# A streaming encoder step on one core: first weight quarter loaded one K tile at a time, fourteen products of ones at the start

## The chip, the cores and the metric

The kernel runs on one core of a Trainium2 chip. A core has a matrix engine (TensorE, PE in the profile, its weight loads PEld), a vector engine (VectorE, DVE), an activation engine (ScalarE, ACT), a general engine (GpSimd, POOL) and a synchronizing engine (SyncE, SP), each with its own instruction queue, and 16 DMA engines. The metric is the device time of one execution in microseconds (us), as the median of several.

## The reference, cut to what matters

One layer of a hybrid encoder for 512 prompt tokens and 8 x 16 sample tokens, 640 in all. Everything is float32.

```
h = rmsnorm(x) @ w_in              # 2048 -> 8448, split into u, z_a, q, k, v, z_b, g_a, g_b
branch_A = GLU(gelu(S5(u))) * silu(z_a)
branch_B = attention(q, k, v) * silu(z_b)
y = x + (sig(g_a) * (branch_A @ w_out_a) + sig(g_b) * (branch_B @ w_out_b)) @ w_o
```

The change lies in the first thing computed: the products of x with the first two blocks of 128 columns of w_in (the first quarter of u). The row factor of the norm is applied to the results, so these products can start before the sums of squares are known.

## The kernel before, in words

All weight matrices are cut into 102 units of 128 x 2048 numbers. A unit of w_in's first eight holds 16 K tiles of 128 x 128. A product in full precision is made of three products in a rounded format: each operand is split into a high part (its rounded value) and a low part (what the rounding left), and hi*hi, lo*hi and hi*lo are added in PSUM. ScalarE makes w_hi by a copy from the raw weights, GpSimd makes w_lo = raw - w_hi, both for every unit. For x, ScalarE makes x_hi (with the norm's gain), and VectorE makes x_lo. x is 16 tiles of 128 x 640, kept for all the input units.

The first three units are handled by quarters of 512 columns, that is of four K tiles. SyncE's queue (L363 to L372) issues, for each quarter, the quarter of unit 0, that of unit 1, and four x tiles; then the quarters of unit 2, each once the old content of its buffer has been split. Units 3 and later go whole.

ScalarE's loop over the 16 x tiles (L997 on) copies the two weight quarters at k = 0, 4, 8, 12, then x_hi of the tile; from k = 8 on it adds the square of x tile k - 8 (`SQ_LAG`). After the loop come the squares of tiles 8 to 11, then the two copies that empty the accumulators of units 0 and 1 (`u_raw`, they raise `acc_free`), the last quarter of unit 2, and the squares of 12 to 15. A square waits for VectorE's running sum two tiles back. VectorE's loop makes x_lo of tile k and from k = 8 on adds the square of tile k - 8 to `ssum`; then come the last eight sums. GpSimd makes the w_lo quarters in the order of the loads (`low`, L451).

TensorE (L521 on) goes over the 16 K tiles of units 0 and 1 together: six products of 320 columns for each unit and tile, weights stationary. It waits for the unit's w_lo quarter (`part_split`, for the last one `w_split`) and for x_lo of the tile (`x_split`). Then unit 2 runs alone and has first to wait for `acc_free` 1. At its tile 8 `norm_sums` multiplies the finished `ssum` with a 128 x 128 tile of ones; from that the roots come on VectorE and ScalarE, and behind the roots in ScalarE's queue stands the copy of unit 3's weights. All later units follow on TensorE one after the other.

The semaphores that the change renumbers are `part_hi` (quarters copied by ScalarE), `part_split` (quarters split by GpSimd) and `x_loaded[k]` (16 for each transfer). `prep` counts GpSimd's two fills, `ones` first.

Of the kernel before, what the change touches and what calls it, by code (L numbers as in the profile page):

```python
# [59 lines left out]
U_ZG = 22  # L60
ZGS = 3
SQ_LAG = 8
SSM_BANK = (6, 7, 5, 6)
KV_BANK = (0, 1, 4, 2, 3)
BRB_AT = ((), (), (0, 1), (2, 3), (4, 5), (6, 7), (), ())
# [25 lines left out]
def build(nc, xT, gain, wts, cst, onehot, rel_tab, sinks, sinks_s, a_re, a_im, log_dt, b_re, b_im, c_re, c_im,  # L91
# [150 lines left out]
    with ctx:  # L242
# [114 lines left out]
        @block.sync  # L357
        def _(spe):
            def load(n, slot):
                spe.dma_start(raw[slot][:], wts[ds(n, 1)].rearrange("a p n -> (a p) n")).then_inc(w_loaded[slot], 16)  # L360

            for q in range(4):
                for p in range(2):  # L363
                    spe.dma_start(raw[p][:, quarter(q)], wts[p][:, quarter(q)]).then_inc(part_loaded[2 * q + p], 16)
                for k in range(4 * q, 4 * q + 4):
                    spe.dma_start(x_raw[:, k, :], xT[k]).then_inc(x_loaded[k], 16)
            for q in range(4):
                if q < 3:
                    spe.wait_ge(part_split, 2 * q + 1)
                else:  # L370
                    spe.wait_ge(w_split, 1)
                spe.dma_start(raw[0][:, quarter(q)], wts[2][:, quarter(q)]).then_inc(part_loaded[8 + q], 16)  # L372
            for t, src in ((tab, rel_tab), (hot, onehot)):
                spe.dma_start(t[:], src).then_inc(small_loaded, 16)
            spe.wait_ge(w_split, 2)
            load(3, 1)
            for t, src in ((sp["are"], a_re), (sp["aim"], a_im), (bre, b_re), (bim, b_im), (cre, c_re),
                           (cim, c_im), (dsk, dskip), (bcol, bglu), (qgc, qg), (kgc, kg),
                           (ident, cst[0]), (diag, cst[2][:, 0:CH])):
                spe.dma_start(t[:], src).then_inc(ssm_loaded, 16)  # L380
            for g2 in range(2):
                spe.dma_start(sp["dt"][64 * g2:64 * g2 + 64, :],
                              log_dt[g2:g2 + 1, :].broadcast_to([64, PAIRS])).then_inc(ssm_loaded, 16)
                spe.dma_start(sk[64 * g2:64 * g2 + 64, :], sinks[g2:g2 + 1, :].broadcast_to([64, 8])).then_inc(ssm_loaded, 16)
            for h in range(8):
                spe.dma_start(skS[16 * h:16 * h + 16, :], sinks_s[h:h + 1, :].broadcast_to([16, 2])).then_inc(ssm_loaded, 16)

            def next_unit(n, p):
                spe.wait_ge(w_split, n - 1)
                load(n, p)  # L390

            spe.wait_ge(prep, 2)
            for kv in range(2):
                spe.dma_start(k_scr[kv, :, 0:PAD], zeros[0:HD, :]).then_inc(pads_stored, 16)
            spe.dma_start(v_scr[0:PAD, :], zeros[:]).then_inc(pads_stored, 16)
            for p in range(2):
                next_unit(4 + p, p)
            spe.wait_ge(rel_copied, 1)
            spe.dma_start(f_scr, fsb[:].unsqueeze(1).broadcast_to([16, QC, RELW])).then_inc(f_stored, 16)

            def store_c(i):

                spe.wait_ge(mats_ready, i + 1)
                for r in range(2):
                    for g2 in range(2):
                        spe.dma_start(c_scr[r].rearrange("p (j a) n -> a p j n", a=2)[g2][:, ds(BLK * i, BLK)],
                                      powers[64 * g2:64 * g2 + 64, :, 0, r, CH:(STEP + 1) * CH]).then_inc(c_stored, 16)

            def load_u(s):
                spe.dma_start(U[16 * (7 - s):16 * (8 - s)],  # L410
                              u_scr.rearrange("t (g c) (s k) -> s c (t g) k", g=8, s=STEP)[s]).then_inc(u_loaded, 16)

            for n in range(6, 18):
                next_unit(n, n % 2)
                if n in C_AT:
                    store_c(C_AT.index(n))
            spe.wait_ge(blk_stored, 32 * 4)
            spe.wait_ge(c_stored, 64 * 4)
            for p in range(2):
                spe.wait_ge(u_stored[p], 64)  # L420
            for p in range(2):
                for s in range(4 * p, 4 * p + 4):
                    load_u(s)
                next_unit(18 + p, p)
            for b in range(2):
                spe.dma_start(Bst[b][:], b_scr[:, BLK * b:BLK * b + BLK]).then_inc(bst_loaded[b], 16)
            with spe.Fori(10, U_G // 2 + 1) as i:
                for p in range(2):
                    next_unit(2 * i + p, p)
            with spe.Fori(0, 7) as c:  # L430
                for k in range(4):
                    next_unit(U_G + 2 + 4 * c + k, k % 2)
                spe.wait_ge(y_done, c + 1)
                stage_h(spe.dma_start, c + 1)
                spe.wait_ge(gelu_stored, 128 * c + 128)
                load_y(spe.dma_start, c + 1)
            with spe.Fori(U_G // 2 + 15, N_UNITS // 2) as i:
                for p in range(2):
                    next_unit(2 * i + p, p)


        @block.gpsimd
        def _(pool):

            for k, (part, value) in enumerate(((ones[:], 1.0), (zeros[:], 0.0))):
                if k:
                    pool.wait_ge(prep, k)
                nc.gpsimd.memset(part, value).then_inc(prep, 1)

            def low(p, cols=slice(0, D)):  # L450
                return nc.gpsimd.tensor_tensor(w_lo[p][:, cols], raw[p][:, cols], w_hi[p][:, cols].bitcast(F32),  # L451
                                               ALU.subtract)

            pool.wait_ge(prep, 2)
            for q in range(4):
                for p in range(2):
                    if q < 3:
                        pool.wait_ge(part_hi, 2 * q + p + 1)
                    else:
                        pool.wait_ge(w_hi_done, p + 1)  # L460
                    low(p, quarter(q)).then_inc(part_split if q < 3 else w_split, 1)
            for q in range(4):
                if q < 3:
                    pool.wait_ge(part_hi, 6 + q + 1)
                else:
                    pool.wait_ge(w_hi_done, 3)
                low(0, quarter(q)).then_inc(part_split if q < 3 else w_split, 1)
            pool.wait_ge(w_hi_done, 4)
            low(1).then_inc(w_split, 1)
            with pool.Fori(2, N_UNITS // 2) as i:  # L470
                for p in range(2):

                    pool.wait_ge(w_hi_done, 2 * i + p + 1)
                    low(p).then_inc(w_split, 1)
# [3 lines left out]
        def _(pe):  # L478
# [32 lines left out]

            def parts_of_unit2(k):
                if k in (0, 4, 8):
                    pe.wait_ge(part_split, 6 + k // 4 + 1)
                if k == 12:
                    pe.wait_ge(w_split, 3)
                if k == 8:
                    norm_sums()


            for k in range(KT):  # L521
                for p in range(2):
                    if k in (0, 4, 8):
                        pe.wait_ge(part_split, 2 * (k // 4) + p + 1)
                    if k == 12:
                        pe.wait_ge(w_split, p + 1)
                    pe.wait_ge(x_split, k + 1)
                    last = k_tile(acc(p), p, k, 0, KT, x_tiles)
                    if k == KT - 1:
                        last.then_inc(proj_done, 1)  # L530
                    elif k % 4 == 3 and p == 0:
                        last.then_inc(part_used, 1)
# [429 lines left out]
        def _(act):  # L962
            def A(out, in_, func, **kw):
                return nc.scalar.activation(out, in_, func, **kw)  # L964
# [30 lines left out]
                    A(sq[k % 2][:], x_raw[:, k, :], ACT.Square).then_inc(x_sq, 1)  # L995

            for k in range(KT):  # L997
                if k % 4 == 0:
                    q = k // 4
                    for p in range(2):  # L1000
                        act.wait_ge(part_loaded[2 * q + p], 16)
                        A(w_hi[p][:, quarter(q)], raw[p][:, quarter(q)], ACT.Copy).then_inc(part_hi if q < 3 else w_hi_done, 1)
                if k >= KT - 2:
                    hi_part2(k - KT + 2)
                if k == 0:
                    act.wait_ge(gain_loaded, 16)
                act.wait_ge(x_loaded[k], 16)
                A(x_hi[:, k, :], x_raw[:, k, :], ACT.Copy, scale=gcol[:, k:k + 1]).then_inc(x_hi_done, 1)
                if k >= SQ_LAG:
                    square_x(k - SQ_LAG)  # L1010
# [1080 lines left out]
```

## Time and profile before

| | us |
|---|---|
| median of 3 runs (lowest, highest) | 1533.71 (1533.5, 1534.25) |
| the profiled execution | 1534.2 |
| its span | 1532.4 |
| TensorE busy | 1520.2 |
| VectorE busy | 654.0 |
| GpSimd busy | 483.9 |
| ScalarE busy | 425.9 |

The span goes from the first to the last instruction; the execution's own time has 1.8 us more around it. A matmul's end is modelled, so records overlap; what counts is the distance between their starts. A row of the timeline may merge several like instructions (x4) and gives in brackets how long the engine was idle before and what ended that.

### The profile page before, as it was taken

How to read it: one execution, taken by the hardware profiler on the slowest of the kernel's cores; microseconds unless marked ns; L12 is line 12 of the kernel's file. 1: busy time of each engine (PE TensorE's matmuls, PEld its weight loads, DVE VectorE, ACT ScalarE, POOL GpSimd, SP SyncE). 2: the span in 40 equal slices, each digit the busy share in tenths (PEclk: the TensorE clock that was granted, in tenths of full speed). 3: DMA queues.
4: the chain of work that ended last, by engine and by line, in shares of the span. 5: the costliest groups of instructions: out<-in, count | busy, mean ns of one | idle time of the engine just before them, and what ended most of it. 6: DMA issues, size and time to landing. Idle time of an engine off the chain costs nothing.

```text
span 1532.4 us, 21441 instructions
## 1 busy us (share of the span) xinstructions
PE 1520.2 (99%) x8377; PEld 1289.6 (84%) x8377; DVE 654.0 (43%) x1049; ACT 425.9 (28%) x582; POOL 483.9 (32%) x117
## 2 busy tenths in 40 slices
PE   7999999999999999999999999999999999999999
PEld 7999888998888878887787877879988888888887
DVE  7897771238776142433424334256522232500000
ACT  7412332421211314323332332434411112311110
POOL 4333232323323232322322323224323333333331
PEclk9999999999999999999999999999999999999999
DMA  7524449743324454464545555446424414342340
GB/s 279 143 76 161 138 141 178 227 142 105 117 83 138 135 147 120 113 164 136 136 114 136 137 145 138 123 167 228 152 83 151 151 56 150 117 151 83 127 148 35
DMA packets 169361, 209.60 MB, mean 137 GB/s; under 512 B 107825, under 2 KB 127569, under 8 KB 155601
## 3 DMA queue, kind: packets, MB, share of 16 engines
q1 hardware_dynamic: 63840, 133.85, 28.8%
q10 hardware_dynamic: 105456, 74.83, 16.6%
q8 instruction: 48, 0.79, 0.2%
q14 instruction: 17, 0.13, 0.0%
HBM read 163.25 MB, written 42.76 MB: 134 GB/s over the span
## 4 chain that ended last, share of the span: by engine, by line
PE 98%; issue 1%; POOL 0%; DMA 0%; DVE 0%; ACT 0%; SPq 0%; POOLq 0%; ACTq 0%
PE ps L795 43%; PE ps L931 14%; PE ps L484 14%; PE ps L798 11%; PE ps L581 9%; PE ps L708 1%; PE ps L717 1%; PE ps L734 1%; PE ps L688 1%; PE ps L732 1%; PE ps L756 1%; PE ps L562 1%; PE ps L724 0%; POOL w_lo L451 0%; PE ps L739 0%
## 5 line engine op out<-in xcount | busy, mean ns | idle before, releaser
L451 POOL TENSOR_TENSOR w_lo<-raw,w_hi 128x2048 fp32r<-128x2048 f32 (+1 forms) x111 | 483.3, 4356 | 1023.8 <-ACT w_hi L964 1023.8
L964 ACT ACTIVATE w_hi<-raw 128x2048 fp32r<-128x2048 f32 (+1 forms) x111 | 197.3, 1778 | 626.3 <-PE ps L798 356.8
L795 PE MATMUL ps<-x_hi,w_hi 128*128 128x512 f32 x704 | 281.9, 400 | 0.0
L795 PE MATMUL ps<-x_lo,w_hi 128*128 128x512 f32 x704 | 274.4, 390 | 0.0
L795 PE MATMUL ps<-x_hi,w_lo 128*128 128x512 f32 x704 | 274.3, 390 | 0.0
L795 PEld LDWEIGHTS ps<-x_hi,w_hi 128*128 128x128 f32 x704 | 132.2, 188 | 30.0 <-issue 1.8
L795 PEld LDWEIGHTS ps<-x_hi,w_lo 128*128 128x128 f32 x704 | 132.1, 188 | 28.4
L795 PEld LDWEIGHTS ps<-x_lo,w_hi 128*128 128x128 f32 x704 | 132.3, 188 | 26.0
L931 PE MATMUL ps<-w_hi,mix_hi 128*128 128x512 f32 x320 | 124.6, 389 | 0.0
L931 PE MATMUL ps<-w_hi,mix_lo 128*128 128x512 f32 x320 | 124.5, 389 | 0.0
L931 PE MATMUL ps<-w_lo,mix_hi 128*128 128x512 f32 x320 | 124.5, 389 | 0.0
L484 PE MATMUL ps<-x_hi,w_hi 128*128 128x320 f32 x384 | 89.5, 315 | 8.6 <-DVE x_lo L1499 8.4
L1992 DVE TENSOR_TENSOR Y<-ps,Y 128x512 f32<-128x512 f32 x20 | 13.6, 692 | 188.0 <-PE ps L931 188.0
L1972 DVE TENSOR_TENSOR gate_in<-ps,gate_in 128x512 f32<-128x512 f32 x40 | 26.7, 692 | 151.8 <-PE ps L795 151.8
L484 PE MATMUL ps<-x_lo,w_hi 128*128 128x320 f32 x384 | 88.5, 312 | 0.0
L484 PE MATMUL ps<-x_hi,w_lo 128*128 128x320 f32 x384 | 88.4, 312 | 0.0
L964 ACT ACT_TABLE_LOAD x37 | 47.5, 1283 | 144.9 <-issue 79.1
L581 PE MATMUL ps<-w_hi,x_hi 128*128 128x512 f32 (+1 forms) x240 | 85.4, 356 | 0.0
L581 PE MATMUL ps<-w_hi,x_lo 128*128 128x512 f32 (+1 forms) x240 | 84.9, 354 | 0.0
L581 PE MATMUL ps<-w_lo,x_hi 128*128 128x512 f32 (+1 forms) x240 | 84.9, 354 | 0.0
L484 PEld LDWEIGHTS ps<-x_hi,w_hi 128*128 128x128 f32 x384 | 65.0, 191 | 9.2 <-POOL w_lo L451 8.8
L1856 DVE SCALAR_TENSOR_TENSOR Sb<-ps,bias 128x768 f32<-128x768 f32 x16 | 15.3, 958 | 133.1 <-PE ps L717 133.1
(267 smaller groups left out, 2535.2 us busy)
## 6 DMA issues: line engine op xcount, KB each, us to landing
raw<-in_wts SPq DMA_DIRECT2D x99, 1024.0 KB, 5.0
g_scr<-gbuf ACTq DMA_DIRECT2D x8, 1024.0 KB, 8.1
gate_in<-g_scr ACTq DMA_DIRECT2D x8, 1024.0 KB, 6.2
x_raw<-in_xT SPq DMA_DIRECT2D x16, 320.0 KB, 8.3
Y<-in_x_tok ACTq DMA_DIRECT2D x20, 256.0 KB, 4.7
out_y_tok<-Y ACTq DMA_DIRECT2D x20, 256.0 KB, 2.8
c_scr<-powers SPq DMA_DIRECT2D x16, 256.0 KB, 4.3
b_scr<-bT ACTq DMA_DIRECT2D x4, 1024.0 KB, 5.7
```

Of the source, the lines that this page charges most:

```text
L451: return nc.gpsimd.tensor_tensor(w_lo[p][:, cols], raw[p][:, cols], w_hi[p][:, cols].bitcast(F32), ALU.subtract)
L484: last = nc.tensor.matmul(outs[:, h, :], w[p][:, c:c + P], act[k][:, h * HALF:(h + 1) * HALF], start=(k == 0 and w is w_hi and act is hi), ...
L562: last = nc.tensor.transpose(ps[:, SSM_BANK[part], (2 * j + ri) * P:(2 * j + ri + 1) * P], powers[:, 2 * part + j, 1, ri, 0:P], ident[:])
L581: last = nc.tensor.matmul(out, act, w[p][:, c:c + width], start=(k == 0 and act is hi and w is w_hi), stop=(k == KT - 1 and act is lo))
L688: last = nc.tensor.matmul(ps[64 * g2:64 * g2 + 64, 4 + 2 * (b % 2) + j // 2, col:col + NCH], Bst[b // 2 % 2][:, 4 * (b % 2) + j, ri, 64 * ...
L708: last = nc.tensor.matmul(out, mat[:, g, m:m + HD], src[:, g, :], start=mat is Mst, stop=mat is Cst)
L717: last = nc.tensor.matmul(ps[:, 5 + r, j * BAND:(j + 1) * BAND], Qp[rows, 2 * j:2 * j + 2, :].rearrange("p a q -> p (a q)"), Kb[rows], sta ...
L795: last = nc.tensor.matmul(ps[:, bank, :], w[p][:, col + P * i:col + P * i + P], act[:, 0:PROMPT], start=opens, stop=final and w is w_lo)
L798: last = nc.tensor.matmul(ps[:, bank, :], act[:, PROMPT:TOK], w[p][:, col:col + WB], start=opens, stop=final and w is w_lo)
L931: last = nc.tensor.matmul(ps[:, t, :], act, w[p][:, c:c + WB], start=(k == 0 and act is hi and w is w_hi), stop=(k == KT - 1 and act is lo))
L964: return nc.scalar.activation(out, in_, func, **kw)
L1972: v.tensor_tensor(g, ps[:, (5 * h + i) % 8, :], g, ALU.mult).then_inc(out_free, 1)
```

## The change

The first quarter of units 0 and 1 is no longer loaded, copied and split as 512 columns, but as four pieces of 128 columns, one for each K tile. SyncE issues piece k of unit 0, piece k of unit 1 and x tile k, for k = 0 to 3; ScalarE copies the two pieces and then x_hi; GpSimd splits eight pieces of 128 columns; TensorE waits for each piece. Pieces 1 to 3 share the semaphore of their x tile, which then counts 48. All later counts are raised accordingly. And ahead of its first operands TensorE makes fourteen products of the tile of ones with itself (128 columns, plain float32) into a PSUM bank that nothing reads, as soon as `prep` is 1.

```diff
+WARM = 14
...
-            for q in range(4):
+            for k in range(4):
+                for p in range(2):
+                    spe.dma_start(raw[p][:, P * k:P * k + P], wts[p][:, P * k:P * k + P]).then_inc(
+                        x_loaded[k] if k else part_loaded[p], 16)
+                spe.dma_start(x_raw[:, k, :], xT[k]).then_inc(x_loaded[k], 16)
+            for q in range(1, 4):
                 for p in range(2):
                     spe.dma_start(raw[p][:, quarter(q)], wts[p][:, quarter(q)]).then_inc(part_loaded[2 * q + p], 16)
                 for k in range(4 * q, 4 * q + 4):
                     spe.dma_start(x_raw[:, k, :], xT[k]).then_inc(x_loaded[k], 16)
             for q in range(4):
                 if q < 3:
-                    spe.wait_ge(part_split, 2 * q + 1)
+                    spe.wait_ge(part_split, 2 * q + 7)
...
             pool.wait_ge(prep, 2)
-            for q in range(4):
+            for k in range(4):
+                for p in range(2):
+                    pool.wait_ge(part_hi, 2 * k + p + 1)
+                    low(p, slice(P * k, P * k + P)).then_inc(part_split, 1)
+            for q in range(1, 4):
                 for p in range(2):
                     if q < 3:
-                        pool.wait_ge(part_hi, 2 * q + p + 1)
+                        pool.wait_ge(part_hi, 2 * q + p + 7)
...
-                    pool.wait_ge(part_hi, 6 + q + 1)
+                    pool.wait_ge(part_hi, 12 + q + 1)
...
                 if k in (0, 4, 8):
-                    pe.wait_ge(part_split, 6 + k // 4 + 1)
+                    pe.wait_ge(part_split, 12 + k // 4 + 1)
...
+            pe.wait_ge(prep, 1)
+            for i in range(WARM):
+                nc.tensor.matmul(ps[:, 7, 0:P], ones[:], ones[:], start=True, stop=True)
             for k in range(KT):
                 for p in range(2):
-                    if k in (0, 4, 8):
-                        pe.wait_ge(part_split, 2 * (k // 4) + p + 1)
+                    if k < 4:
+                        pe.wait_ge(part_split, 2 * k + p + 1)
+                    if k in (4, 8):
+                        pe.wait_ge(part_split, 2 * (k // 4) + p + 7)
...
             for k in range(KT):
-                if k % 4 == 0:
+                if k < 4:
+                    if k:
+                        act.wait_ge(x_loaded[k], 48)
+                    for p in range(2):
+                        if k == 0:
+                            act.wait_ge(part_loaded[p], 16)
+                        A(w_hi[p][:, P * k:P * k + P], raw[p][:, P * k:P * k + P], ACT.Copy).then_inc(part_hi, 1)
+                elif k % 4 == 0:
...
-                act.wait_ge(x_loaded[k], 16)
+                if k == 0 or k > 3:
+                    act.wait_ge(x_loaded[k], 16)
```

## Rows read from the trace of the kernel before

**Rows 1.** The page: its head, and busy us, share and instructions of TensorE.
```profile
span 1532.4 us, 21441 instructions
PE 1520.2 (99%) x8377; PEld 1289.6 (84%) x8377; DVE 654.0 (43%) x1049; ACT 425.9 (28%) x582; POOL 483.9 (32%) x117
```

**Rows 2.** The page: the chain that ended last, by engine.
```profile
PE 98%; issue 1%; POOL 0%; DMA 0%; DVE 0%; ACT 0%; SPq 0%; POOLq 0%; ACTq 0%
```

**Rows 3.** Waits of TensorE, whole span: us in total, times, longest.
```profile
PE ps L484 <- DVE x_lo L1499: 8.4, 1, 8.4
```

**Rows 4.** Windows: length, PE busy (records), granted clock, DMA share, GB/s.
```profile
0.00:8.42 8.42, 0.00 (x0) 1.00 0.72 244
8.42:14.30 5.88, 5.88 (x22) 1.00 1.00 370
14.30:38.50 24.20, 24.20 (x166) 1.00 0.76 267
```

**Rows 5.** Timeline of TensorE: start us, length us, instruction, count.
```profile
8.42 0.87 PE L484 MATMUL ps<-x_hi,w_hi 128*128 128x320 f32 x2 [8.42 <-DVE x_lo L1499]
...
39.46 0.56 PE L484 MATMUL ps<-x_hi,w_hi 128*128 128x320 f32 x2
...
47.22 1.34 PE L508 MATMUL ps<-ssum,ones 128*128 128x320 f32 x4
48.40 1.17 PE L541 MATMUL ps<-ones,ssum 128*128 128x1 f32 x10
...
56.87 0.56 PE L484 MATMUL ps<-x_hi,w_hi 128*128 128x320 f32 x2
```

**Rows 6.** Timeline of ScalarE.
```profile
4.33 1.31 ACT L964 ACTIVATE w_hi<-raw 128x512 fp32r<-128x512 f32 x2 [2.09 <-DMA raw<-in_wts]
6.26 3.21 ACT L964 ACTIVATE x_hi<-x_raw,gcol 128x640 fp32r<-128x640 f32 x4 [0.62 <-DMA x_raw<-in_xT]
9.67 0.63 ACT L964 ACTIVATE w_hi<-raw 128x512 fp32r<-128x512 f32 x1 [0.20 <-DMA raw<-in_wts]
...
16.51 0.83 ACT L964 ACTIVATE x_hi<-x_raw,gcol 128x640 fp32r<-128x640 f32 x1 [0.20 <-DMA x_raw<-in_xT]
...
37.16 0.74 ACT L964 ACTIVATE sq<-x_raw 128x640 f32<-128x640 f32 x1 [0.19 <-DVE ssum L1491]
38.70 0.71 ACT L964 ACTIVATE u_raw<-ps 128x640 f32<-128x640 f32 x1 [0.80 <-PE ps L484]
39.58 0.70 ACT L964 ACTIVATE u_raw<-ps 128x640 f32<-128x640 f32 x1 [0.17 <-PE ps L484]
```

**Rows 7.** Timeline of VectorE.
```profile
17.37 2.63 DVE L1499 SCALAR_TENSOR_TENSOR x_lo<-x_raw,gcol,x_hi 128x640 fp32r<-128x640 f32 x2 [1.26 <-ACT x_hi L964]
...
22.19 0.88 DVE L1499 SCALAR_TENSOR_TENSOR x_lo<-x_raw,gcol,x_hi 128x640 fp32r<-128x640 f32 x1
...
23.82 1.82 DVE L1499 SCALAR_TENSOR_TENSOR x_lo<-x_raw,gcol,x_hi 128x640 fp32r<-128x640 f32 x1
...
32.61 1.92 DVE L1499 SCALAR_TENSOR_TENSOR x_lo<-x_raw,gcol,x_hi 128x640 fp32r<-128x640 f32 x1
34.46 4.53 DVE L1491 TENSOR_TENSOR ssum<-ssum,sq 128x640 f32<-128x640 f32 x5
```

**Rows 8.** Timeline of GpSimd.
```profile
0.74 0.20 POOL L448 MEMSET ones<- 128x128 f32 x1 [0.29 <-POOLq L2067]
...
5.11 2.49 POOL L451 TENSOR_TENSOR w_lo<-raw,w_hi 128x512 fp32r<-128x512 f32 x2 [3.90 <-ACT w_hi L964]
...
22.62 6.02 POOL L451 TENSOR_TENSOR w_lo<-raw,w_hi 128x512 fp32r<-128x512 f32 x3 [4.09 <-ACT w_hi L964]
28.85 1.62 POOL L451 TENSOR_TENSOR w_lo<-raw,w_hi 128x512 fp32r<-128x512 f32 x1 [0.21 <-ACT w_hi L964]
...
52.18 4.64 POOL L451 TENSOR_TENSOR w_lo<-raw,w_hi 128x2048 fp32r<-128x2048 f32 x1 [9.99 <-ACT w_hi L964]
```

**Rows 9.** Timeline of SyncE's queue.
```profile
1.65 1.85 SPq L366 DMA_DIRECT2D x_raw<-in_xT  x4
```

**Rows 10.** DMA: x tile 3; unit 2's last quarter; issues at 32.04 and 32.52.
```profile
x_raw<-in_xT SPq DMA_DIRECT2D x1, 320.0 KB, 5.5
...
raw<-in_wts SPq DMA_DIRECT2D x1, 256.0 KB, 3.0
...
kgc<-in_kg SPq DMA_DIRECT2D x1, 0.5 KB, 3.6
ident<-in_cst SPq DMA_DIRECT2D x1, 64.0 KB, 3.3
```

## The prediction

> **What bounds the kernel now.** I read the engine shares first: TensorE (PE) is busy for 1520.2 of the span's 1532.4 us [rows 1], and the chain that ended last is TensorE for 98% [rows 2]. The table of waits has one single wait on the PE row: 8.4 us, the very first, until the first x_lo tile [rows 3]. So whatever the change brings must be a shift of TensorE's whole stream, and it is worth what the stream is earlier by at the first place behind which everything hangs on TensorE itself.
>
> Then the windows: from 8.42 to 14.30 us TensorE starts 22 products of 320 columns in 5.88 us, 267 ns apart; from 14.30 to 38.50 it starts 166 in 24.20 us, 146 ns apart [rows 4]. 320 columns in 267 ns is the lower level, 1.2 GHz; in 146 ns nearly the upper, 2.4 GHz. The granted clock stands at 1.00 in both rows, so only the spacing shows it. The engine had done nothing before. Those 22 products cost 22 x 0.121 = 2.7 us more than they would at the upper level.
>
> Last, the first 60 us engine by engine, because TensorE alone does not say how far the others are behind it. The first product of unit 2 stands at 39.46 [rows 5]. It needs accumulator 0, which ScalarE empties at 38.70 for 0.71 us, after waiting 0.80 us for TensorE [rows 6]. In ScalarE's queue the four squares of x tiles 8 to 11 stand directly ahead of this copy; the last runs from 37.16 to 37.90 and waits for VectorE's running sum [rows 6]. VectorE in turn is busy without a gap that matters from 17.37 to 38.99: x_lo 15 runs 32.61 to 34.53 and five sums 34.46 to 38.99 [rows 7]. It is slow because GpSimd runs its three w_lo of the last quarter and of unit 2 in the same stretch: an x_lo takes 1.82 or 1.92 us there against 0.88 elsewhere [rows 7, 8]. What starts that chain is not TensorE: x_hi 8 at 16.51 came 0.20 us after a wait for its own transfer [rows 6].
>
> **The parts.**
>
> *TensorE's first operands.* They need w pieces 0 of both units and x tile 0. Bytes queued ahead of the end of x tile 0 fall from 256+256+320 KB to 64+64+320 KB. x_hi 0 begins at 6.26 now and TensorE at 8.42, so 2.16 us lie behind the transfer [rows 5, 6]. How much earlier x tile 0 lands no row shows. If bytes set it, 384 KB fewer are worth 1.0 us at the 370 GB/s of the second stretch and 1.6 at the 244 of the first [rows 4]; if the queue's start-up sets it, nothing. I take 1.1 us, since the queue moved bytes all the while: first operands at 7.3 (6.8 to 8.4).
>
> *Fourteen products of ones.* ones is written at 0.94 [rows 8]. Two 320-column products of plain f32 (four records) take 48.40 - 47.22 = 1.18 us at the upper level [rows 5], so 128 columns cost 0.24 us, and 0.43 at the lower level (x 267/146). Fourteen take 3.3 to 6.0 us and end by 7.1, before the operands. They delay nothing. In the trace the level rose 5.9 us after the first product, so 1.1 + 5.9 = 7.0: nearly all of the 2.7 us should be saved.
>
> *Feeding tiles 1 to 15.* At 12 x 0.147 = 1.76 us per K tile, TensorE would want tile k at 7.3 + 1.76k and finish unit 1 at 35.5. ScalarE's two 512-column copies (0.65 each) become eight of 128 columns, at most 0.36 each; GpSimd's two at 1.25 become eight of about 0.43, by the slope between 512 and 2048 columns (4.64 - 1.25 over 1536) [rows 6, 8]. Both fall between x tiles that come 0.8 us or more apart, on engines idle here: ScalarE ended tile 3 at 9.47 and waited for the next quarter, so they cost nothing unless that cover of 0.2 us and the following waits is gone. Up to tile 12 nothing is late. But x_lo 15 ends at 34.53 [rows 7] and is wanted at 33.7: here TensorE starts to wait again, about 1.3 us with d (below) and the 0.14 from x_lo to product.
>
> *The six extra transfers.* SyncE issues 12 instead of 6 before quarter 1, 0.46 us each ([rows 9], four in 1.85 us): its queue moves back 2.8 us. x tile 3 is issued near 0.74 + 11 x 0.5 = 6.3 instead of 3.07, when it lands at 3.07 + 5.5 = 8.6 [rows 10]. A 256 KB transfer issued into a nearly empty queue landed after 3.0 us [rows 10]; with 0.2 for the larger size tile 3 comes at 9.5 at the latest, 0.9 late. From quarter 1 on the transfers stand back to back again and can make none of it up, or some. Small packets cost something too: kgc (landed 3.6 after 32.04) and ident, 64 KB (landed 3.3 after 32.52) are 0.2 us apart, so 64 KB in 512-byte rows take 0.2 us or a little more; eight take 1.9 where two of 256 KB took 1.4 (512 KB at 370 GB/s). Together tiles 4 to 15 come 0 to 0.9 us later (the idle moments of the queue and the 0.5 overlap); between the ends I take d = 0.4. The later issues (unit 2's quarters, unit 3, the SSM constants) wait for GpSimd's counts anyway and keep their times within d.
>
> *Where it is paid out.* ScalarE cannot empty accumulator 0 before the square of tile 11 is done: 37.90 + d. TensorE's first product of unit 2 came 0.76 us after that copy's start (39.46 - 38.70), so it comes at 38.66 + d = 39.06 instead of 39.46. TensorE's unit 1 now ends about 34.9 + 0.1 + 1.8 = 36.8, and it stands still for over 2 us. Of 3.9 us earned, 0.80 - d = 0.4 is left. Even with no products of ones at all the number would be the same: 8.42 - 7.3 = 1.1 is already more than 0.4.
>
> *After it.* Everything later hangs on TensorE. The sums of squares for the norm (47.22) feed the root, the copy of unit 3's weights and its w_lo (52.18 to 56.82), and unit 3 starts at 56.87, as soon as that is done [rows 5, 8]: this chain begins at TensorE's own product, so it moves by the same 0.4. The sum of squares itself is ready earlier by about 1 us, since the copy of accumulator 1 (39.58 now) no longer waits for TensorE either.
>
> Sum: profiled execution 1534.2 - 0.80 + 0.4 = 1533.8 us. That execution is 0.5 above the median of the three, 1533.71, which would give 1533.3; about halfway, 1533.5, is the forecast.
>
> **A rule weighed.** VectorE's and GpSimd's slow instructions: x_lo 12 takes 1.82 and the four w_lo in 22.62 to 30.48 take 1.6 to 2.3 instead of 1.25 [rows 7, 8]. The Trainium skill, "SBUF — State Buffer", section "Who interferes with whom", says that a VectorE operation with two SBUF inputs and a GpSimd one that reads SBUF share a port pair as an exclusive lock, and the second fully blocks. By that rule the slowness cannot be shortened by feeding TensorE differently, and the eight small w_lo only add chances of a block on x_lo 0 to 3, off the path. By that rule the sum stays; if instead the two shared without blocking, VectorE's chain could shorten and rival 1 would come in. The trace agrees in kind with the rule: the slow instructions on both engines lie where the two run together.
>
> **Rivals.**
> 1. *The stream really moves.* If VectorE meets GpSimd less often, the squares end early enough. With the squares out of the way but x_lo 15 at 34.53 + d, accumulator 0 is complete at 35.0 + 6 x 0.147 + 0.1 = 36.0, and unit 2 starts 0.76 later at 36.8: 2.7 us gained, 1531.5 by the profiled execution. Without that either: 35.5, 3.9 gained, 1530.3. For it: no row of PE waits; against: the w_lo in this stretch and VectorE's gapless row, which no edit shortens; one meeting more or less is 0.94 us (1.82 - 0.88), and three fewer would be needed.
> 2. *The new gap costs the clock.* TensorE stands still for 2.2 us ahead of unit 2 and 1.3 at tile 15, where it had no idle time. Before its first product, an idle engine ran 22 products slowly. If it falls again, unit 2 pays 22 x 0.121 = 2.7 us: 1533.5 + 2.7 = 1536.2, slower than before by 0.16%, and beyond 0.2% if more than 27 products are slow (1536.8). From 3 slow products on it outweighs the 0.4 gained. Against it: the gap is much shorter than the 8.4 us of idle at the start.
> 3. *The queue pays.* d reaches 0.9 or 1.2, beyond its bounds: the whole chain of VectorE is later and the kernel loses 0.1 to 0.4: 1533.8 to 1534.1.
> 4. *The products of ones do not lift the clock.* Then accumulator 0 is complete 1.1 earlier than now, at 37.6, still hidden behind 37.90 + d: 1533.5. It is a case of no change in the time, but the trace would differ.
>
> **How the numbers follow.** The forecast (with 4) 0.62; rival 3 0.16; rival 1 0.13, of which 0.09 beyond 0.2%, and I add 0.02 for what I don't see; rival 2 0.09, of which 0.04 beyond. A change of 0.2% is 3.07 us, about what a measurement of this kernel can tell from none; below 1530.6 is faster, above 1536.8 slower. Chances: faster 0.11, same 0.84, slower 0.05. The forecast's own range is 1532.4 to 1534.2 (d from 0 to 0.9 about either basis, one collision less). For 8 in 10 I go down to rival 1's first form and up into rival 2: 1531.4 to 1535.0.
>
> **What would show it.** First product of ones near 1.1, the first tile's products from about 7.3 and 146 ns apart within a microsecond; x_hi 8 at 16.5 to 17.4; square 11 ending at 37.9 + d; a PE wait of about 2 us, released by ScalarE's u_raw, and the first product of unit 2 near 39.1; unit 3 at 56.5. The prediction is wrong if the copy of accumulator 0 starts before 37.5, if the spacing in unit 2 is 267 ns, or if a later wait swallows the 0.4.

## The result, and the profile after

| | before | after |
|---|---|---|
| median of 20 runs, us | 1533.99 | 1537.42 |
| lowest, highest | 1533.37, 1535.06 | 1535.41, 1538.99 |
| the profiled execution, its span | 1534.2, 1532.4 | 1537.12, 1535.3 |

The ratio is 1.0022, 95% interval 1.0016 to 1.0028: the change makes the kernel 3.4 us slower. 1533.5 was forecast, with a range up to 1535.0. The runs also spread over 3.6 us instead of 1.7.

The page after: its head and busy times. TensorE has 28 records more, the products of ones (two each).

```profile
span 1535.3 us, 21521 instructions
PE 1525.0 (99%) x8405; PEld 1293.1 (84%) x8405; DVE 656.0 (43%) x1049; ACT 425.8 (28%) x588; POOL 481.8 (31%) x123
```

The waits of TensorE's row in the changed kernel (total us, times, longest), against the one wait of [rows 3]; 1.0 us until the tile of ones is there and 0.2 us much later are not shown:

```profile
PE ps L494 <- DVE x_lo L1522: 3.3, 4, 1.1
PE ps L494 <- ACT u_raw L979: 1.9, 1, 1.9
```

The same windows as [rows 4], and one more (length, PE busy and records, granted clock, DMA share, GB/s):

```profile
0.00:8.42 8.42, 6.40 (x38) 1.00 0.70 196
8.42:14.30 5.88, 4.82 (x34) 1.00 0.95 325
14.30:38.50 24.20, 22.85 (x152) 1.00 0.83 295
38.50:60.00 21.50, 19.44 (x117) 0.92 0.19 56
```

The start did what it was to do, and the time was still lost. There are three things to see. TensorE works early, but its waits are new. The transfers move 196 GB/s up to 8.42 and 325 up to 14.30, where they moved 244 and 370 [rows 4]. x tile 3 was issued at 5.93 and landed after 4.8 us, at 10.75 (8.62 before):

```profile
x_raw<-in_xT SPq DMA_DIRECT2D x1, 320.0 KB, 4.8
```

And the granted clock is 0.92 in the last window, behind unit 1.

TensorE's timeline after (start, length, instruction, idle before), against [rows 5]:

```profile
1.00 4.87 PE L533 MATMUL ps<-ones 128*128 128x128 f32 x28 [1.00 <-POOL ones L454]
6.89 0.53 PE L494 MATMUL ps<-x_hi,w_hi 128*128 128x320 f32 x2 [1.02 <-DVE x_lo L1522]
...
36.67 0.56 PE L494 MATMUL ps<-x_hi,w_hi 128*128 128x320 f32 x2 [0.55 <-DVE x_lo L1522]
...
40.63 0.56 PE L494 MATMUL ps<-x_hi,w_hi 128*128 128x320 f32 x2 [1.94 <-ACT u_raw L979]
...
42.08 0.73 PE L494 MATMUL ps<-x_lo,w_hi 128*128 128x320 f32 x2
...
45.20 0.46 PE L494 MATMUL ps<-x_lo,w_hi 128*128 128x320 f32 x2
...
49.93 1.34 PE L518 MATMUL ps<-ssum,ones 128*128 128x320 f32 x4
```

First operands at 6.89 instead of 8.42, and all of unit 1 at the upper level (records of two products are 0.46 or 0.53 long, not 0.73). Tile 15 waits at 36.67 for x_lo. Then TensorE stands still for 1.94 us until ScalarE has emptied accumulator 0, and unit 2 starts at 40.63, 1.17 us later than the 39.46 of [rows 5]. One microsecond into unit 2 twelve products come 267 ns apart (the row at 42.08 is 0.73 long), at the lower of the two levels; at 45.20 the spacing is the short one again. The norm sums stand at 49.93 instead of 47.22: 2.71 us late, of which 1.17 from unit 2's start and 1.5 from the clock. The span is 2.9 us longer. Nothing behind them gives anything back.

ScalarE's and VectorE's rows after, against [rows 6] and [rows 7]:

```profile
13.28 3.32 ACT L979 ACTIVATE x_hi<-x_raw,gcol 128x640 fp32r<-128x640 f32 x4 [0.18 <-DMA x_raw<-in_xT]
...
18.25 0.83 ACT L979 ACTIVATE x_hi<-x_raw,gcol 128x640 fp32r<-128x640 f32 x1 [0.20 <-DMA x_raw<-in_xT]
...
39.25 0.74 ACT L979 ACTIVATE sq<-x_raw 128x640 f32<-128x640 f32 x1 [0.19 <-DVE ssum L1514]
39.89 1.28 ACT L979 ACTIVATE u_raw<-ps 128x640 f32<-128x640 f32 x2
```
```profile
14.14 7.95 DVE L1522 SCALAR_TENSOR_TENSOR x_lo<-x_raw,gcol,x_hi 128x640 fp32r<-128x640 f32 x6 [1.22 <-ACT x_hi L979]
...
34.70 1.92 DVE L1522 SCALAR_TENSOR_TENSOR x_lo<-x_raw,gcol,x_hi 128x640 fp32r<-128x640 f32 x1
36.54 4.53 DVE L1514 TENSOR_TENSOR ssum<-ssum,sq 128x640 f32<-128x640 f32 x5
```

The two copies at 39.89 have no idle time before them: they waited in the queue behind the square at 39.25, no longer for TensorE. That square was at 37.16. VectorE starts x_lo 4 at 14.14, and six of them take 7.95 us without a gap; without a meeting with GpSimd they would take 6 x 0.8 = 4.8, so three of the six are long ones. Singly, x_lo 4, 7 and 8 read:

```profile
14.14 1.88 DVE L1522 SCALAR_TENSOR_TENSOR x_lo<-x_raw,gcol,x_hi 128x640 fp32r<-128x640 f32 x1 [1.22 <-ACT x_hi L979]
17.54 1.92 DVE L1522 SCALAR_TENSOR_TENSOR x_lo<-x_raw,gcol,x_hi 128x640 fp32r<-128x640 f32 x1
19.38 1.92 DVE L1522 SCALAR_TENSOR_TENSOR x_lo<-x_raw,gcol,x_hi 128x640 fp32r<-128x640 f32 x1
```

A meeting here means that VectorE's instruction and GpSimd's w_lo run at the same time. In the kernel before only one of the same six was long, x_lo 8. Its rows for x_lo 4 to 9 are these, with 2.03 and 1.26 us of idle time, and GpSimd's for quarters 1 and 2:

```profile
12.70 3.41 DVE L1499 SCALAR_TENSOR_TENSOR x_lo<-x_raw,gcol,x_hi 128x640 fp32r<-128x640 f32 x4 [2.03 <-ACT x_hi L964]
```
```profile
10.38 2.66 POOL L451 TENSOR_TENSOR w_lo<-raw,w_hi 128x512 fp32r<-128x512 f32 x2 [2.78 <-ACT w_hi L964]
15.75 2.78 POOL L451 TENSOR_TENSOR w_lo<-raw,w_hi 128x512 fp32r<-128x512 f32 x2 [2.70 <-ACT w_hi L964]
```

After, GpSimd's stand at

```profile
12.61 2.73 POOL L457 TENSOR_TENSOR w_lo<-raw,w_hi 128x512 fp32r<-128x512 f32 x2 [0.56 <-ACT w_hi L979]
17.19 3.42 POOL L457 TENSOR_TENSOR w_lo<-raw,w_hi 128x512 fp32r<-128x512 f32 x2 [1.85 <-ACT w_hi L979]
```

that is on x_lo 4 and on x_lo 7 and 8. The two engines did not move together: GpSimd's quarter 1 starts 2.23 us later and x_lo 4 only 1.44; its quarter 2 starts 1.44 us later and x_lo 7 (15.24 before) 2.30. The small w_lo did not hold quarter 1 up. GpSimd was idle for 0.56 us ahead of it, waiting for ScalarE's copy, which stood at 11.91 behind x_hi 3 (11.19), and that waited for x tile 3.

### The profile page after: what moved, and what is told of

Same layout as the page of the kernel before. It is cut to its first block, busy times and chain, and to the rows that moved or that the text cites. A ratio compares the mean times of both kernels' runs of the same rounds, so it can differ in the third digit from the quotient of the medians.

```text
span 1535.3 us, 21521 instructions
## 1 busy us (share of the span) xinstructions
PE 1525.0 (99%) x8405; PEld 1293.1 (84%) x8405; DVE 656.0 (43%) x1049; ACT 425.8 (28%) x588; POOL 481.8 (31%) x123
## 4 chain that ended last, share of the span: by engine, by line
PE 88%; DVE 7%; issue 2%; DMA 1%; SPq 1%; POOL 0%; ACT 0%; DVEq 0%; POOLq 0%
PE ps L810 43%; PE ps L946 14%; PE ps L813 11%; PE ps L494 8%; PE ps L596 6%; DVE pt L1533 3%; PE ps L723 1%; PE ps L732 1%; DVE powers L1533 1%; DVE powers L1612 1%; DMA c_scr<-powers 1%; PE ps L749 1%; DVE ssum L1514 1%; PE ps L703 1%; PE ps L747 1%
## 5 line engine op out<-in xcount | busy, mean ns | idle before, releaser
L457 POOL TENSOR_TENSOR w_lo<-raw,w_hi 128x2048 fp32r<-128x2048 f32 (+2 forms) x117 | 481.2, 4116 | 1028.7 <-ACT w_hi L979 1028.7
L979 ACT ACTIVATE w_hi<-raw 128x2048 fp32r<-128x2048 f32 (+2 forms) x117 | 198.0, 1696 | 625.7 <-PE ps L813 369.0
L810 PEld LDWEIGHTS ps<-x_hi,w_hi 128*128 128x128 f32 x704 | 132.2, 188 | 30.0 <-issue 1.8
L946 PEld LDWEIGHTS ps<-w_lo,mix_hi 128*128 128x128 f32 x320 | 60.1, 188 | 12.5
```

The source lines that it names most:

```text
L810: last = nc.tensor.matmul(ps[:, bank, :], w[p][:, col + P * i:col + P * i + P], act[:, 0:PROMPT], start=opens, stop=final and w is w_lo)
L946: last = nc.tensor.matmul(ps[:, t, :], act, w[p][:, c:c + WB], start=(k == 0 and act is hi and w is w_hi), stop=(k == KT - 1 and act is lo))
```

## The experiments

The versions e1 to e10 have 11 runs each, beside runs of the kernel before; "long" is the number of VectorE's instructions up to x_lo 15 that take over 1.5 us. The trace's columns are of one execution each. The kernel before had medians of 1533.91 beside e1 to e4, 1533.93 beside e5 to e8 and 1533.57 beside e9 and e10.

| kernel | x tile 8 lands | long | square 11 ends | unit 2 starts | norm sums | median us | ratio (95%) |
|---|---|---|---|---|---|---|---|
| before | 16.48 | 6 | 37.90 | 39.46 | 47.22 | 1533.99 | |
| after | 18.22 | 8 | 39.98 | 40.63 | 49.93 | 1537.42 | 1.0022 (1.0016 to 1.0028) |
| e1, ones only | 16.54 | 6 | 38.01 | 38.66 | 46.42 | 1534.85 | 1.0008 (0.9999 to 1.0017) |
| e2, pieces only | 18.66 | 8 | 40.45 | 41.10 | 50.41 | 1536.47 | 1.0015 (1.0006 to 1.0024) |
| e3, after + 9 ones between | 17.86 | 8 | 40.06 | 40.71 | 48.48 | 1536.15 | 1.0014 (1.0005 to 1.0023) |
| e4, pieces from ScalarE's queue | 15.93 | 8 | 39.28 | 39.92 | 47.69 | 1536.00 | 1.0018 (1.0009 to 1.0027) |
| e5, zeros as w_lo | 17.91 | 0 | 34.66 | 36.44 | 44.20 | 1531.91 | 0.9988 (0.9979 to 0.9997) |
| e6, new order + 24 ones | 16.66 | 5 | 38.89 | 36.98 | 44.75 | 1532.41 | 0.9991 (0.9982 to 1.0000) |
| e7, new order only | 16.25 | 5 | 41.37 | 39.29 | 47.05 | 1533.91 | 0.9999 (0.9990 to 1.0008) |
| e8, 24 ones + 8 between | 17.81 | 8 | 39.62 | 40.27 | 48.04 | 1533.86 | 0.9999 (0.9990 to 1.0008) |
| e9, first piece only | 17.80 | 10 | 41.14 | 39.34 | 47.10 | 1534.28 | 1.0008 (0.9999 to 1.0017) |
| e10, after + new order | 18.42 | 7 | 40.66 | 38.74 | 46.51 | 1534.20 | 1.0005 (0.9995 to 1.0014) |

**e1 and e2: the two parts alone.** e1 is the kernel before plus

```diff
+WARM = 14
...
+            pe.wait_ge(prep, 1)
+            for i in range(WARM):
+                nc.tensor.matmul(ps[:, 7, 0:P], ones[:], ones[:], start=True, stop=True)
```

and e2 the changed kernel without these lines.

> The kernel before with the fourteen products of ones alone, quarters as before. Theory A (the whole loss comes from the pieces: they make x tile 8 land 1.74 us later, 18.22 instead of 16.48, and the squares of tiles 8 to 11 stand ahead of the copy that frees accumulator 0): the square of tile 11 ends at 37.9 as before, unit 2 starts at 38.7, the kernel is 0.8 us faster than before, 1533.2, unless the clock falls in the gap ahead of unit 2 (about 2.0 us, TensorE done with unit 1 at 36.6) or between the ones (5.9) and the first operands (8.4), which costs up to 1.6 us per fall. Theory B (the products of ones do the harm: they disturb the start's transfers): x tile 8 lands near 18.2 here too and the kernel is 3 us slower than before.

> The changed kernel without the products of ones. Theory A: x tile 8 lands near 18.2 and the square of tile 11 ends near 40.0 as in the changed kernel, unit 2 starts at 40.6, 1.2 us later than before; unit 1 starts at 6.9 at the lower clock and ends later than in the changed kernel, so that the gap ahead of unit 2 is shorter and the clock need not fall: 1535.2. Theory B: transfers as in the kernel before, x tile 8 at 16.5, unit 2 at 38.7: 1533.2.

The traces came as theory A has them: with the ones alone the transfers and VectorE's chain are those of before, and unit 2 starts at 38.66, where the square of tile 11 lets it; with the pieces alone both are late, 41.10. The pieces are the cause of the late chain, the ones are not. TensorE's waits in e1:

```profile
PE ps L485 <- DVE x_lo L1503: 2.7, 1, 2.7
PE ps L485 <- ACT u_raw L968: 1.8, 1, 1.8
```

But e1's median is 0.9 us above the kernel before (1533.2 was expected), though its profiled execution (1533.6) is below it; its runs lie from 1533.6 to 1536.2. The interval of the ratio reaches 0.9999, so a loss by the ones alone is not shown. And in e2 the clock fell in unit 2 although I had expected a gap too short for it: the gap was 1.93 us. In e2 unit 1 started at 6.9 at the lower level, which still brought it to its end at 39.17. Expected was 1535.2, the median is 1536.47.

**e3: the standstill filled.** The changed kernel with

```diff
+FILL = 9
...
+            for i in range(FILL):
+                nc.tensor.matmul(ps[:, 7, 0:P], ones[:], ones[:], start=True, stop=True)
```

between units 1 and 2.

> The changed kernel with nine more products of ones between units 1 and 2, where TensorE stands still for 1.9 us; they take about 2.0 us at the upper clock. Theory A, second part (the standstill makes the granted clock fall for 3.4 us, twelve products 267 instead of 147 ns apart, 1.5 us, in a profiled run): no fall, unit 2 starts at 40.6 as before the addition, norm sums at 48.4 instead of 49.9, median 1535.8 and a narrower spread than 1535.4 to 1539.0. Rival: the fall comes from something else (a pattern of the clock after its early rise) and stays: 1537.4.

Windows of e3 (columns as above), and its timeline around unit 2:

```profile
38.50:60.00 21.50, 21.35 (x145) 1.00 0.23 63
```
```profile
38.61 2.17 PE L551 MATMUL ps<-ones 128*128 128x128 f32 x18
48.48 1.34 PE L519 MATMUL ps<-ssum,ones 128*128 128x320 f32 x4
```

The granted clock stays at 1.00 where it was 0.92. Unit 2 starts as late as before the addition (40.71), but the norm sums come 7.77 us behind it instead of 9.30 (7.76 in the kernel before). The median falls by 1.27 us and the spread from 3.6 to 1.3. One profiled execution would not show that the filling did it, because e4's had the same standstill of 1.94 us and no fall (its timeline, and its window with the granted clock of 1.00):

```profile
39.92 0.41 PE L494 MATMUL ps<-x_hi,w_hi 128*128 128x320 f32 x1 [1.94 <-ACT u_raw L979]
38.50:60.00 21.50, 19.93 (x130) 1.00 0.26 75
```

The mean granted clock of every run says more. Six of e4's eleven runs have 1.000 and lie from 1535.11 to 1536.00; five have 0.999 and lie from 1537.05 to 1537.66. In e2 it is five runs, 1535.4 to 1535.8, against six with less, 1536.5 to 1537.6. In the changed kernel twelve of twenty are below 1.000 (median 1538.1, the other eight 1536.2), in e3 one of eleven. So the standstill costs its own length always, and in some executions the clock after it, some 1.6 to 1.9 us by these groups.

**e4: SyncE's lead given back.** The six pieces of K tiles 1 to 3 are issued from ScalarE's queue, idle at that time, and no longer from SyncE's:

```diff
...
+            for k in range(1, 4):
+                for p in range(2):
+                    act.dma_start(raw[p][:, P * k:P * k + P], wts[p][:, P * k:P * k + P]).then_inc(x_loaded[k], 16)
```

> The changed kernel with the six weight pieces of K tiles 1 to 3 issued from ScalarE's queue instead of SyncE's, so that SyncE issues six transfers before quarter 1 as in the kernel before. Rows and bytes are unchanged. If SyncE's lead was the cause of the late transfers (Q): x tile 3 lands near 8.9 and x tile 8 near 16.9 instead of 18.22, the square of tile 11 ends near 38.7, the median is 1 to 1.3 us lower than the changed kernel's, 1536.2. If the 512-byte rows themselves are (S): x tile 8 stays at 18.0 to 18.3 and the time at 1537.4.

x tile 3 landed at 8.63, as in the kernel before (8.62), and x tile 8 at 15.93, earlier than there, with the same 512-byte rows. So the rows are not the cause. Whether it helped that SyncE kept its lead, or that a second queue took part, this run can't tell apart. But the square of tile 11 still ended at 39.28 and the expected 38.7 was missed: transfers in time were worth 0.7 us only. VectorE's row in e4 shows why:

```profile
13.24 8.14 DVE L1525 SCALAR_TENSOR_TENSOR x_lo<-x_raw,gcol,x_hi 128x640 fp32r<-128x640 f32 x6 [0.88 <-ACT x_hi L979]
```

Six x_lo in 8.14 us again. ScalarE copies the weights of quarter 1 only after x_hi 3, whose piece had landed at 10.19, so GpSimd's work on quarter 1 falls on x_lo 4 and 5 (12.0 to 15.4) and that on quarter 2 on x_lo 6 and 7. In the kernel before it was over at 13.04, before x_lo 4 had ended. This is the second half of d, and it does not need late transfers.

**e5: no meetings.** GpSimd writes zeros instead of computing w_lo, for quarters 1 to 3 of units 0 and 1 and for unit 2; those low parts are left out.

```diff
-                    low(p, quarter(q)).then_inc(part_split if q < 3 else w_split, 1)
+                    fill(p, quarter(q)).then_inc(part_split if q < 3 else w_split, 1)
...
-                low(0, quarter(q)).then_inc(part_split if q < 3 else w_split, 1)
+                fill(0, quarter(q)).then_inc(part_split if q < 3 else w_split, 1)
```

> The changed kernel in which GpSimd writes zeros into w_lo of quarters 1 to 3 of units 0 and 1 and of unit 2, instead of computing raw - w_hi (the low parts of those weights are left out, so that the output is not the reference's). Theory C (VectorE's chain is long because it meets GpSimd's subtractions: 8 of its instructions take 1.9 us instead of 0.85 in the changed kernel, 6 in the kernel before): with nothing to meet, no x_lo or sum takes over 1.2 us, the square of tile 11 ends near 34 although the transfers are as late as in the changed kernel, x_lo 15 ends near 31, unit 2 starts when TensorE and the copy allow, about 36, and the time is near 1537.4 - 4.6 - 1.5 = 1531.3. Rival D (the late transfers alone set it, and the slow instructions are an effect of waiting): the square of tile 11 stays near 40 and the time at 1537.4.

VectorE's and GpSimd's rows in e5:

```profile
14.14 3.37 DVE L1525 SCALAR_TENSOR_TENSOR x_lo<-x_raw,gcol,x_hi 128x640 fp32r<-128x640 f32 x4 [2.03 <-ACT x_hi L982]
18.80 0.88 DVE L1525 SCALAR_TENSOR_TENSOR x_lo<-x_raw,gcol,x_hi 128x640 fp32r<-128x640 f32 x1 [1.28 <-ACT x_hi L982]
...
30.34 0.89 DVE L1525 SCALAR_TENSOR_TENSOR x_lo<-x_raw,gcol,x_hi 128x640 fp32r<-128x640 f32 x1 [0.25 <-ACT x_hi L982]
```
```profile
24.03 1.05 POOL L461 MEMSET w_lo<- 128x512 f32 x2 [5.71 <-ACT w_hi L982]
```

The transfers are as late as in the changed kernel (17.91) and x_lo 4 starts at the same 14.14, but no instruction is long, VectorE has gaps of 1.28 and 0.25 us, and the square of tile 11 ends 5.3 us earlier. Unit 2 starts at 36.44 and the median is 5.5 us below the changed kernel's. The slow instructions are a cause, not an effect: all eight are gone here, also the six that the kernel before has, so the 5.3 us are not the price of the two new ones. Expected were 34, 36 and 1531.3. GpSimd also works less here (two fills in 1.05 us against two w_lo in 2.73), so this shows what the meetings cost together with GpSimd's time, not one by one.

**e6, e7: the order in ScalarE's queue.** Loads by quarters as before; the copies that free the accumulators go ahead of squares 10 to 15 and the last quarter of unit 2 behind them. e6 has 24 products of ones besides.

```diff
-            for k in range(KT - SQ_LAG, KT - 4):
+            for k in range(KT - SQ_LAG, KT - 6):
                 square_x(k)
             for p in range(2):
                 act.wait_ge(proj_done, p + 1)
                 A(halves(u_raw[p][:]), acc(p), ACT.Copy).then_inc(acc_free, 1)
-            hi_part2(3)
-            for k in range(KT - 4, KT):
+            for k in range(KT - 6, KT):
                 square_x(k)
+            hi_part2(3)
```

> The kernel before, loads by quarters, with 24 products of ones ahead of the first operands (to about 7.5) and another order in ScalarE's queue: squares of tiles 8 and 9, then the two copies that free the accumulators, then squares 10 to 15, then the last quarter of unit 2. Theory A (the squares in front of the copy are what holds unit 2): accumulator 0 is complete at 35.8 (x_lo 15 at 34.6), unit 2 starts near 36.7 instead of 39.46, norm sums at 44.3 if the sum of squares (expected at 43.5) does not hold them, no clock fall: 1531.2, 2.7 us faster than before. Rival E (the sum of squares is late by the new order and holds the norm sums): norm sums after 45.5 and a gain below 1.5 us.

> The kernel before with the new order in ScalarE's queue alone. Theory A: TensorE is still the later one (accumulator 0 complete at 38.66), so unit 2 starts at 39.4 as before; 1533.9, no change. If the order alone were the gain, it would be as fast as the run with 24 products of ones.

ScalarE's and TensorE's rows in e6:

```profile
35.59 0.74 ACT L968 ACTIVATE sq<-x_raw 128x640 f32<-128x640 f32 x1 [1.84 <-DVE ssum L1495]
36.24 1.41 ACT L968 ACTIVATE u_raw<-ps 128x640 f32<-128x640 f32 x2
```
```profile
36.98 0.57 PE L485 MATMUL ps<-x_hi,w_hi 128*128 128x320 f32 x2
...
44.75 1.34 PE L509 MATMUL ps<-ssum,ones 128*128 128x320 f32 x4
```

Unit 2 starts 2.48 us earlier than before, as expected, and the norm sums keep it; the sum of squares ends at 43.77, in time. e7 alone changes nothing (1533.91), also as expected: then TensorE is the later one. The profiled execution of e6 is 2.0 us below that of the kernel before, its median 1.5 below, where 2.7 were expected. Its interval just reaches 1; it is the only version that computes everything and has a median over 0.1 us below the kernel before. Of the 2.47 us that it is ahead at the norm sums 2.04 are left at the span's end. The rest goes at 184.17, where TensorE waits for VectorE, which it does not do in the kernel before:

```profile
PE ps L618 <- DVE kvb L1725: 0.5, 1, 0.5
```

Neither half of e6 gives this alone: e7 gives nothing, and the ones alone (e1) start unit 2 at 38.66.

**e8: both standstills filled.** e1 with 24 products of ones ahead and 8 between units 1 and 2.

> The kernel before with 24 products of ones ahead and 8 between units 1 and 2, ScalarE's order as before. The run with 14 and none between had unit 2 at 38.66 and 1533.6 in its profiled execution but a median of 1534.85 and a spread of 2.6 us. Theory A, second part (that spread is the granted clock falling in some executions, in the two standstills of 2.7 and 1.8 us): with the standstills filled every execution is like the profiled one: median 1533.3, spread below 1.3 us. Rival: the spread has another cause and stays near 2.6 us.

The median is 1.0 us below e1's (1533.3 was expected), but the spread stays at 2.4: half right. All eleven runs have a mean granted clock of 1.000, where six of e1's eleven have less, so the spread that is left has another cause. The profiled execution (1535.2) shows one: x tile 0 landed at 7.13 (6.17 before) and x tile 8 at 17.81, though the loads were those of the kernel before, and VectorE had 8 long instructions. So a kernel that loads by quarters can have late transfers too, here in one of five profiled executions. The kernels with all pieces in SyncE's queue had them in all five (17.86 to 18.66). What delays a start by quarters stays open.

**e9, e10.** e9 is e6 with K tile 0 alone split off, 18 products of ones and the squares two tiles later:

```diff
+            for p in range(2):
+                spe.dma_start(raw[p][:, 0:P], wts[p][:, 0:P]).then_inc(part_loaded[p], 16)
+            spe.dma_start(x_raw[:, 0, :], xT[0]).then_inc(x_loaded[0], 16)
...
-SQ_LAG = 8
+SQ_LAG = 10
```

e10 is the changed kernel with the order of e6.

> The version with ScalarE's new order and products of ones (18 here), with K tile 0 alone split off from the first quarter (two transfers of 64 KB, the rest of the quarter as two of 192 KB: two more transfers, not six), and the squares two tiles later (SQ_LAG 10), so that VectorE finishes x_lo earlier. Theory A with C: SyncE keeps its lead, x tile 4 lands by 12.3, first operands at 7.0, x_lo 15 near 32.5, unit 2 near 35.7, and the sum of squares, bound by VectorE's whole work, holds the norm sums at 43.5 or later: 0.5 to 1.2 us faster than the version it starts from, 1531.4. If the two extra transfers cost what six did, VectorE meets GpSimd twice more and it is 1 us slower, 1533.4.

> The changed kernel (all pieces, 14 products of ones) with ScalarE's new order. Theory A: the copy no longer waits for squares 10 and 11, so unit 2 follows x_lo 15 (36.6 in the changed kernel): 38.7 instead of 40.63, the standstill ahead of unit 2 falls from 1.9 us to 0.1 and with it the clock fall: 1537.4 - 1.9 - 1.3 = 1534.2, still 1.8 us behind the same order with loads by quarters (1532.4), which is what late transfers and meetings cost. Rival: if the order gained only because x_lo 15 was early, the changed kernel gains under 1 us.

e9 fell on its second branch and worse: x tile 1 landed at 8.47 (6.98 before), 10 instructions were long, x_lo 15 ended at 35.33, and the median is 0.7 us above the kernel before, where e6 is 1.5 below. Its one row for eleven x_lo:

```profile
10.18 14.73 DVE L1525 SCALAR_TENSOR_TENSOR x_lo<-x_raw,gcol,x_hi 128x640 fp32r<-128x640 f32 x11 [3.57 <-ACT x_hi L981]
```

e10 came out at the expected numbers: 38.74 for 38.7, and 1534.20 for 1534.2, without a fall of the clock. It is 0.6 us above the kernel before beside it, where the changed kernel is 3.4 above and e6 1.5 below: the order gives back 2.8 us, and the pieces still cost 2.1, with unit 2 (38.74 against 36.98) bound to x_lo 15, which ends at 36.59.

## Why the prediction was wrong

- *The path* was right. The square of tile 11 frees accumulator 0, unit 2 starts 0.65 us behind the square's end in the changed kernel and in e1 (0.76 was said), and all the rest moves with the norm sums. In e1 and e10 unit 2 started within 0.1 us of the times worked out from it.
- *First operands and ones.* 7.3 was said, 6.89 measured; the clock rose near 4.1, not 7.0. Both better than said, and both worth nothing, as said. Missed: the ones ended at 5.9 and, with one tile's operands there and the next late, TensorE waited for x_lo 1 until 9.95.
- *The six extra transfers: the step that failed.* d was put at 0.4 between 0 and 0.9; it is 2.08 (39.98 - 37.90). It has two parts. x_lo 4 starts 1.44 us later (14.14 instead of 12.70), since x tile 4 lands 1.44 us later: the bound of 0.9 came from one transfer issued alone and took the queue to be full again at once, and it was not: x tile 3 landed at 10.75, where 9.5 was called the latest, 4.8 us after its issue instead of 3.2 (9.94 to 11.36 in e2, e3, e5 and e10). Second, two meetings more with GpSimd, 1.9 us (x_lo 4 takes 1.88 instead of 1.02, x_lo 7 1.92 instead of 0.87). Against them stands 1.26 us in which VectorE had been idle ahead of x_lo 8 [rows 7]: 1.44 + 1.9 - 1.26 = 2.1. I had the price of a meeting (0.94) and the rows where they lie, but let the number of meetings stand, and so moved a chain in one piece whose two engines moved by different amounts (2.23 and 1.44 us at quarter 1, 1.44 and 2.30 at quarter 2). Either half alone uses up that idle time; e4, without the late transfers, gained 0.7 only.
- *Rival 2, the clock*, had 0.09 and came in, on top: twelve slow products, 1.5 us, where 22 and 2.7 were priced. It was judged by the 8.4 us of idle at the start; it came behind 1.94 us, with 0.55 at tile 15 and 1.06 and 0.70 at tiles 1 and 4, and not in every execution. That the standstill brings it rests on e3 and on the clocks of the single runs (e4, e2). The long queue of rival 3 and the clock of rival 2 belong together, as the later square makes the standstill; I had given them as alternatives.
- *The rule on the shared port pair* holds as far as e5 goes: with a GpSimd instruction that only writes, VectorE's are never long. The Trainium skill, "SBUF — State Buffer", section "Who interferes with whom", says just that of instructions that only write. What was drawn from it here was too little: it looked at the small w_lo alone, which in fact cost nothing on the path, and not at where the large ones of quarters 1 and 2 would fall. They came onto x_lo 4, 7 and 8, late by ScalarE's copy and not by the small ones.
- *The sum.* 1533.8 by the profiled execution; with 2.08 for 0.4 it is 1535.5, with the clock's 1.5 it is 1537.0, and 1537.1 was measured.

## What to carry to other kernels

Before a start is made earlier, ask which queue the next wait hangs on: here an in-order queue held the copy that frees an accumulator behind squares that nothing needed yet, and moving it made the early lift of the clock worth something (e6, 1.5 us less by the median), while moving it alone (e7) brought nothing and starting early in pieces alone (e2) lost 2.6 us. When a chain is moved, move both engines that meet on it separately and count the meetings again; and count the idle time in it, which absorbs the first of two delays but not both. A faster stage in front of an unmoved wait turns work into a standstill, and a standstill of TensorE may cost its clock too, in some executions and not in others: one profile that looks clean does not rule it out.

## What the runs showed of the hardware

- TensorE's granted clock fell about 1 us after a standstill of 1.94 us had ended, in the middle of dense work, from 41.7 to 45.1. After standstills of 1.94 us (e4), 1.89 (e9, at 11.88) and 1.78 (e1) the profiled executions showed no fall. The runs of the changed kernel spread from 1535.4 to 1539.0, with the standstill filled from 1535.5 to 1536.7.
- The products of ones brought the upper level 2.9 to 6.2 us after the first of them (at 1.00): 3.92 in e1, 4.13 in the changed kernel, 7.21 in e9.
- x tile 8 landed 1.4 to 2.2 us later, with the same bytes ahead of it, when SyncE issued twelve transfers instead of six for them, and not late (15.93) when six of the twelve went through ScalarE's queue. It was also late, 17.80, with eight transfers (e9), and once with six (e8, 17.81), so the number of transfers is not the only cause.
